# Seven-product pairs of a SwiGLU input stage: ScalarE's order (seed, SiLU, last difference), VectorE's first-pair order and two PSUM banks changed

## What is computed

```python
def swiglu(x, w_in, w_out):
    a, b = jnp.split(x @ w_in, 2, axis=-1)      # w_in: 1024 x 5632
    return (jax.nn.silu(a) * b) @ w_out
for i in range(2):
    h = h + 0.5 * swiglu(rmsnorm(h, g_ff1[i]), w_ff1_in[i], w_ff1_out[i])
    ...
    h = h + 0.5 * swiglu(rmsnorm(h, g_ff2[i]), w_ff2_in[i], w_ff2_out[i])
```

## Time and profile before

| | us |
|---|---|
| median of 3 runs | 2997.67 (2995.54 to 3002.64) |
| profiled execution, its own time | 2998.98 |
| its span | 2997.0 |
| TensorE busy / VectorE / ScalarE / GpSimd | 2900.9 / 2123.1 / 1396.3 / 455.9 |
| mean granted TensorE clock, share of full | 0.988 |

### The profile page before, as it was taken

One profiled execution on the slowest core, in us unless ns is written; L12 is line 12 of the kernel. 1 busy time (PEld: TensorE's weight loads), 2 busy tenths in 40 slices (PEclk: granted clock), 3 DMA queues, 4 the chain that ended last, 5 costly groups with the idle time before them and its releaser, 6 DMA issues. The chain is left out here.

```text
span 2997.0 us, 50791 instructions
## 1 busy us (share of the span) xinstructions
PE 2900.9 (97%) x18548; PEld 2500.2 (83%) x18548; DVE 2123.1 (71%) x3185; ACT 1396.3 (47%) x2309; POOL 455.9 (15%) x356
## 2 busy tenths in 40 slices
PE   7999999889999999999999999999999999999998
PEld 3888888777789988777799988799888777899886
DVE  5677776355689745887699845899547886899545
ACT  3645555454356522334466522566323335566422
POOL 0113112184600011000300012100110000200012
PEclk9999999999999999999999999999999999999998
DMA  6212022123223222322232323233222222323322
GB/s 258 62 44 63 24 55 59 36 81 117 99 88 112 97 98 81 98 92 77 98 107 98 115 88 112 71 112 99 100 89 92 92 78 87 110 98 112 104 95 74
DMA packets 97244, 275.10 MB, mean 92 GB/s; under 512 B 35712, under 2 KB 36864, under 8 KB 95760
## 3 DMA queue, kind: packets, MB, share of 16 engines
q1 hardware_dynamic: 94016, 267.89, 27.3%
q10 hardware_dynamic: 2768, 4.25, 0.5%
q0 software_dynamic: 320, 1.05, 0.1%
HBM read 267.88 MB, written 5.28 MB: 91 GB/s over the span
## 5 line engine op out<-in xcount | busy, mean ns | idle before, releaser
L142 DVE TENSOR_TENSOR weights_lo<-weights_raw,weights_hi 128x1024 fp32r<-128x1024 f32 (+2 forms) x258 | 397.6, 1541 | 326.2 <-ACT weights_hi L137 322.7
L137 ACT ACTIVATE weights_hi<-weights_raw 128x1024 fp32r<-128x1024 f32 (+2 forms) x250 | 285.3, 1141 | 431.8 <-PE bank L151 424.7
L149 PE MATMUL bank<-x_hi,weights_hi 128*128 128x512 f32 x832 | 336.9, 405 | 4.6 <-DVE x_lo L1943 2.7
L151 PE MATMUL bank<-x_hi,weights_lo 128*128 128x512 f32 x832 | 326.4, 392 | 0.0
L150 PE MATMUL bank<-x_lo,weights_hi 128*128 128x512 f32 x832 | 325.2, 391 | 0.0
L2053 PE MATMUL bank<-sum_hi,block_hi 128*128 128x256 f32 x960 | 271.2, 282 | 13.7 <-ACT bank L2194 9.6
L149 PE MATMUL bank<-hidden_hi,weights_hi 128*128 128x512 f32 x704 | 273.9, 389 | 0.0
L150 PE MATMUL bank<-hidden_lo,weights_hi 128*128 128x512 f32 x704 | 273.9, 389 | 0.0
L151 PE MATMUL bank<-hidden_hi,weights_lo 128*128 128x512 f32 x704 | 273.9, 389 | 0.0
L2054 PE MATMUL bank<-sum_lo,block_hi 128*128 128x256 f32 x960 | 270.8, 282 | 0.0
L2055 PE MATMUL bank<-sum_hi,block_lo 128*128 128x256 f32 x960 | 269.9, 281 | 0.0
(11 more groups left out here) (437 smaller groups left out, 7322.6 us busy)
## 6 DMA issues: line engine op xcount, KB each, us to landing
raw_pair<-w_ff1in SPq DMA_DIRECT2D x42, 1024.0 KB, 4.9
raw_pair<-w_ff2in SPq DMA_DIRECT2D x42, 1024.0 KB, 4.9
weights_raw<-w_mix SPq DMA_DIRECT2D x72, 512.0 KB, 3.5
weights_raw<-w_ff1out SPq DMA_DIRECT2D x32, 704.0 KB, 4.0
weights_raw<-w_ff2out SPq DMA_DIRECT2D x32, 704.0 KB, 4.1
weights_raw<-w_tail SPq DMA_DIRECT2D x42, 512.0 KB, 3.5
mod_weights<-w_mod SPq DMA_DIRECT2D x6, 2048.0 KB, 16.7
weights_raw<-w_dn SPq DMA_DIRECT2D x24, 512.0 KB, 3.7
```

The source lines that it names most:

```text
L137: nc.scalar.activation(K.wh[:, slot, 0:cols], K.raw[:, slot, 0:cols], ACT.Copy).then_inc(S.wh_ready, 1)
L142: nc.vector.tensor_tensor(K.wl[:, slot, 0:cols], K.raw[:, slot, 0:cols], K.wh[:, slot, 0:cols].bitcast(F32), ALU.subtract).then_inc(S.raw_ ...
L149: nc.tensor.matmul(out, K.wh[:, slot, a:b], xh, start=start, stop=False)
L151: return nc.tensor.matmul(out, K.wl[:, slot, a:b], xh, start=False, stop=stop)
```

## The change

ScalarE's order in each pair becomes seed, SiLU, `fourth_hi`. Pair 3 is taken out of the loop (`second=True`) with the order seed, (for q = 0 the second plain pair's SiLU, `plain_block_hi`, `hidden_hi`), `fourth_hi`, SiLU. The third and fourth plain slabs collect in banks 5 and 3 instead of 3 and 5. On VectorE `second` of pair 3 comes ahead of `first_lo`. For q = 0 both engines' first pairs get an order of their own: `rstd` right after the differences, the gates of the plain pairs later, the table load behind `plain_block_hi`. The table's SiLU writes a column of its own.

```diff
--- before.py
+++ after.py
@@ -319,6 +319,7 @@
     K.ident = put("identity", [128, 128])
     K.ones = put("ones", [128, 128])
     K.eps = put("eps", [128, 1])
+    K.unread = put("unread", [128, 1])
     K.banks = ctx.enter_context(nc.psum_tensor("bank", [128, 4096], F32))
     K.pb = [K.banks[:, 512 * i:512 * i + 512] for i in range(8)]
     return at
@@ -2038,14 +2039,14 @@
         if q > 0:
             pe_sum_squares(pe, q)
         project(1, 4, False)
-        project(2, 3, False)
+        project(2, 5, False)
         if q == 0:
             pe_sum_squares(pe, q)
             K.final_pe(pe)
 
         for bank in (1, 2):
             nc.tensor.matmul(pb[bank][:, :], K.identr[:, :], xgh[:, 0, :], start=True, stop=True)
-        project(3, 5, False)
+        project(3, 3, False)
 
         def product(out, hi, lo, x, start=False):
             for k in range(4):
@@ -2149,7 +2150,7 @@
             nc.scalar.activation(K.t1[:, :], K.t1[:, :], ACT.Silu).then_inc(S.silu_ready, 1)
 
         def silu_table():
-            nc.scalar.activation(K.s5[:, 0:1], K.eps[:, 0:1], ACT.Silu)
+            nc.scalar.activation(K.unread[:, 0:1], K.eps[:, 0:1], ACT.Silu)
 
         def hidden_hi(j):
             act.wait_ge(S.g_ready, FT * f + j + 1 + CREDIT)
@@ -2203,10 +2204,19 @@
             act.wait_ge(S.product_done, left("product_done") + 5 * number(j) + product)
             nc.scalar.activation(half_out(p, name), half_out(p, "a_right"), ACT.Copy).then_inc(S.seeded, 1)
 
-        def half_pair(j, p, end=False):
-            fourth_hi(j)
-            silu(j - 1)
-            seed_a(j, p)
+        def half_pair(j, p, end=False, second=False):
+            if second:
+                seed_a(j, p)
+                if q == 0:
+                    silu(1, True)
+                    plain_block_hi(j, p)
+                    hidden_hi(1)
+                fourth_hi(j)
+                silu(j - 1)
+            else:
+                seed_a(j, p)
+                silu(j - 1)
+                fourth_hi(j)
             keep_fifth(j)
             seed_b(j, p, "b_left", 3)
             hidden_hi(j - 1)
@@ -2224,6 +2234,20 @@
 
             first_hi(j, p, True)
             plain_block_hi(j, p)
+            if q == 0:
+                silu_table()
+                second_hi(j, True)
+                seed_a(j, p)
+                silu(0, True)
+                keep_fifth(j, True)
+                sum_hi(4)
+                seed_b(j, p, "b_left", 3)
+                fourth_hi(j)
+                seed_b(j, p, "b_right", 5)
+                first_hi(j + 1, 1 - p)
+                hidden_hi(0)
+                second_hi(j + 1)
+                return
             silu(0, True)
             second_hi(j, True)
             seed_a(j, p)
@@ -2249,9 +2273,12 @@
             act_std(act, q)
             K.final_act(act)
         sum_hi(3)
-        silu_table()
+        if q > 0:
+            silu_table()
         first_half_pair(PLAIN_PAIRS, 0)
-        with act.Fori(0, HALF_PAIRS // 2 - 1) as i:
+        half_pair(PLAIN_PAIRS + 1, 1, second=True)
+        half_pair(PLAIN_PAIRS + 2, 0)
+        with act.Fori(1, HALF_PAIRS // 2 - 1) as i:
             for p in (1, 0):
                 half_pair(2 * i + PLAIN_PAIRS + 2 - p, p)
         half_pair(FT - 1, 1, end=True)
@@ -2311,13 +2338,13 @@
         def scale_plain(j):
             dve.wait_ge(S.slab_done, s0 + 2 * j + 1 + CREDIT)
             dve.wait_ge(S.g_ready, FT * f + j + CREDIT)
-            nc.vector.tensor_tensor(K.t1[:, :], pb[3 * j][:, :], rstd[:, :], ALU.mult).then_inc(S.evac, 2)
+            nc.vector.tensor_tensor(K.t1[:, :], pb[5 * j][:, :], rstd[:, :], ALU.mult).then_inc(S.evac, 2)
 
         def gate_plain(j):
             dve.wait_ge(S.slab_done, s0 + 2 * j + 2 + CREDIT)
             dve.wait_ge(S.silu_ready, FT * f + j + 1 + CREDIT)
             dve.wait_ge(S.hid_ready, FT * f + j + CREDIT)
-            nc.vector.tensor_tensor(K.t2[:, :], pb[4 + j][:, :], K.t1[:, :], ALU.mult).then_inc(S.g_ready, 1)
+            nc.vector.tensor_tensor(K.t2[:, :], pb[4 - j][:, :], K.t1[:, :], ALU.mult).then_inc(S.g_ready, 1)
 
         def sum_b(j, p, end=False):
             dve.wait_ge(S.slab_done, s0 + 2 * j + (2 if end else 1) + CREDIT)
@@ -2398,13 +2425,34 @@
         def first_half_pair(j, p):
 
             differences(j, p)
+            if q == 0:
+                dve_rstd(dve, q, v0)
+                first_lo(j, p)
+                second(j, p)
+                fourth(j, p)
+                scale_plain(0)
+                second_lo(j)
+                plain_block_lo(j, p)
+                sum_lo(3)
+                sum_lo(4)
+                fourth_lo(j)
+                differences(j + 1, 1 - p)
+                gate_plain(0)
+                first_lo(j + 1, 1 - p)
+                second(j + 1, 1 - p)
+                scale_plain(1)
+                hidden_lo(0)
+                second_lo(j + 1)
+                gate_plain(1)
+                fourth(j + 1, 1 - p)
+                hidden_lo(1)
+                sum_b(j, p)
+                scale_a(j, p)
+                return
             second(j, p)
             fourth(j, p)
-            if q == 0:
-                first_lo(j, p)
             dve_rstd(dve, q, v0)
-            if q > 0:
-                first_lo(j, p)
+            first_lo(j, p)
             scale_plain(0)
             plain_block_lo(j, p)
             gate_plain(0)
@@ -2416,8 +2464,8 @@
             sum_lo(4)
             differences(j + 1, 1 - p)
             fourth_lo(j)
+            second(j + 1, 1 - p)
             first_lo(j + 1, 1 - p)
-            second(j + 1, 1 - p)
             fourth(j + 1, 1 - p)
             hidden_lo(1)
             second_lo(j + 1)
```

## The result

The changed kernel takes 3024.05 us (median; 3020.7 to 3025.27) against 2999.26 for the kernel before (four runs of it, among them the three of the table above), a ratio of 1.0081 with a 95% interval of 1.0064 to 1.0099. The forecast was 2985.0, range 2980.7 to 2991.5. The profiled execution's span is 3021.9 us, 24.9 more than before.

The account below looks back on a forecast made before the run. TensorE, busy 97% of 2997.0 us, bounds the kernel, so only its idle time and slow clock can be won. Gains 5.0 + 2.0 + 3.7 + 2.0 = 12.7 us give 2986.3, less 1.31 for the median 2985.0; range 2980.7 to 2991.5.

Parts of the forecast that it names:

- The waits: Second seven-product pairs and first stage: shorter TensorE waits, gaining 2.0 us in stages 2 and 4, 3.7 in 3, 5.0 in 1.
- PLAIN of pair 3 in stage 1: First stage: PLAIN starts at 844.45 after a new 3.2 us wait on `plain_block_lo`, 6.05 us earlier than before.
- The wait on `plain_block_lo`: Second pair of the three later stages: PLAIN, due at 1527.9, gets a new wait of 0.35 us.
- the 2.39: Second stage, pair 3: SECOND's 2.39 us wait for the seed, which stands behind SiLU, is gone with seed first.
- The slow clock: Half-clock stretch of 3.4 us costs 1.7: charged behind stage 1's new PLAIN wait, gone behind stage 3's second pair.
- The repeated pairs' waits: 72 loop pairs: no TensorE wait, nothing gained or lost; VectorE's idle 0.89 ahead of `second_lo` shrinks to 0.2.
- rival 4: Repeated pairs: gate behind SiLU behind seed, VectorE's cover too thin, 27.5 us lost less 12.7, 3012.5 us; chance 0.04.
- Rival 1: First stage: the new PLAIN wait brings no slow clock, gain 14.4, 2983.3 us; chance 0.18.
- rival 3: Three later stages: VectorE, not the seed, sets SECOND or PLAIN, waits of about 2 remain, gain 5.0, 2992.7 us; chance 0.08.
- rival 2: First stage gives all back through VectorE's single file and missed ScalarE handovers; gain 7.7, 2990.0 us; chance 0.12.
- The table load: First stage, ScalarE: load counted as 1.28 us without the skill's 1.38 drain, which would make the gain 4.7.

Follow-up runs that it names:

- run 2: Changed kernel with all its new order, its extra column moved to free bytes at the top of SBUF: 2988.39 us, ratio 0.9958 to the kernel before.
- run 4: Changed kernel with its extra column widened from 32 to 64 bytes: 2986.19 us, ratio 0.9957 to the kernel before.
- run 9: Changed kernel with its 32-byte column allocated ahead of the weights' buffers instead of behind them: 2982.03 us, ratio 0.9938 to the kernel before.
- run 10: As run 2, with the weights of all seven products at 64 modulo 128: 2963.53 us, ratio 0.9863 to the kernel before.
- run 11: As run 2, with the weights of all seven products at 0 modulo 128: 2990.91 us, ratio 0.9965 to the kernel before.
- run 1: Kernel before plus only an unused 32-byte column behind `eps`, shifting every buffer allocated after it: 3034.68 us against 2999.83, ratio 1.012.
- run 3: Kernel before plus an unused 64-byte column behind `eps`: 3001.73 us, ratio 1.0009.
- run 5: Kernel before with 32 bytes free ahead of `weights_raw`, moving the weights' buffers and everything behind them together: 2997.31 us, ratio 0.9994.
- run 6: Kernel before with only `x_hi` and `x_lo` at 32 modulo 64, all else moved by 0 or 64 bytes: 3020.93 us, ratio 1.007.
- run 7: Kernel before with `block_hi` and `block_lo` moved from 32 to 0 modulo 64 (64 modulo 128), order unchanged: 2981.34 us, ratio 0.9939.
- run 8: Kernel before with only the loop's new ScalarE order, also in pair 3, and the bank swap, memory unshifted: 2992.31 us, ratio 0.9975.

## Why the prediction was wrong, step by step

**The waits: right.** Run 2 shows them without the memory shift. In stages 2 and 4 the start of pair 4 lies 2.24 and 2.28 us earlier behind the stage's first product than before (20.42 for 22.66 and 22.70), 2.0 forecast; in stage 3 3.76 (20.43 for 24.19), 3.7 forecast; in stage 1 5.07 (25.30 for 30.37), 5.0 forecast. PLAIN of pair 3 in stage 1, the longest chain of the prediction, starts 18.00 behind the stage's first product; the prediction's own times give 844.45 - 826.4 = 18.05. Sum 13.3 in the trace, 12.6 in the ratio, 12.7 forecast. Stage 2's second pair in the changed kernel, ScalarE and VectorE, answers to the earlier trace rows:
```profile
1533.87 1.22 DVE L2398 TENSOR_TENSOR block_lo<-differences,block_hi 128x1024 fp32r<-128x1024 f32 x1
...
1534.54 0.58 ACT L2195 ACTIVATE bank<-bank 128x512 f32<-128x512 f32 x1 [1.01 <-PE bank L2056]
...
1536.21 1.22 DVE L2393 TENSOR_TENSOR plain_block_lo<-raw_pair,plain_block_hi 128x1024 fp32r<-128x1024 f32 x1
1536.33 0.63 ACT L2150 ACTIVATE t<-t 128x512 f32<-128x512 f32 x1 [0.67 <-DVE t L2357]
```
The seed no longer stands behind SiLU, and `second_lo` runs in time. The wait on `plain_block_lo`, 0.35 forecast, stands in run 2's timeline as 0.15. The timeline counts idle time from the modelled end of the last matmul, 0.16 after the next one would normally have started, so PLAIN is 0.31 late. The same 0.16 is missing in the 2.39, which delayed SECOND by 2.55; that is why 2.24 was gained where I had summed 2.0.

**The slow clock: right in place, too dear in price, and in stage 3 partly luck.** In stage 1 the wait of 2.92 is followed by one stretch at half clock, as charged; the one behind stage 3's second pair is gone. From the changed kernel's timeline, and its granted clock behind the wait (columns as in the earlier trace rows):
```profile
848.53 0.38 PE L2054 MATMUL bank<-x_hi,plain_block_hi 128*128 128x256 f32 x1 [2.92 <-DVE plain_block_lo L2393]
```
```profile
849.40:852.80 3.40, 3.40 (x18) 3.40 (x18) 3.37 (x7) 1.41 (x2) 0.00 (x0) 0.51 0.91 296
```
That charge was sound: a wait of 2.9 us there comes with one slow stretch in all six traces with the new order of stage 1 (the change, runs 2, 4, 9, 10, 11). Its price was not. I took half of 3.4 us, but by the earlier trace rows the stretch holds 18 or 19 matmuls where 29 fit, so about 10 are lost, 1.2 us; by pair times it costs 1.53 (24.19 - 22.66 before, stage 3 against stage 2). In stage 3 the 0.2 charged too much and the 0.24 of the waits that I had missed cancel, which is why 3.7 met 3.76. And that stage 3 had a slow stretch at all was the draw of one execution: in the six traces that keep the old order (before, runs 1, 3, 5, 6, 7) 10 of the 18 waits on the seed in stages 2 to 4 come with one, from none in run 7 to all three in runs 5 and 6. The 13.3 is a difference from that same trace, so its closeness to 12.7 says less than it seems; the 12.6 from the run times, 9.3 to 16.2, is the independent figure.

**The repeated pairs' waits: right.** Run 2 and the change have no TensorE wait in the loop. VectorE's idle time ahead of `second_lo` fell from 0.89 to 0.18, where 0.2 was forecast, and the gate waits for SiLU instead; another pair of the changed kernel:
```profile
1602.13 1.23 DVE L2398 TENSOR_TENSOR block_lo<-differences,block_hi 128x1024 fp32r<-128x1024 f32 x1 [0.18 <-ACT block_hi L2185]
...
1606.38 0.69 DVE L2362 TENSOR_TENSOR t<-t,t 128x512 f32<-128x512 f32 x1 [0.69 <-ACT t L2150]
```
So rival 4, the only one on the slower side, named the wrong mechanism, though the sign was its own. Rival 1 (no slow clock) and rival 3 (the swap not working) did not happen either; rival 2's chain stayed in time.

**The table load: right by the row.** In the changed kernel too the load (827.88, 1.28 us) is followed at once by the next ACTIVATE:
```profile
827.88 1.28 ACT L2153 ACT_TABLE_LOAD   x1
829.17 0.20 ACT L2153 ACTIVATE unread<-eps 128x1 f32<-128x1 f32 x1
```
The Trainium skill (ScalarE: Activation LUTs, section What ACT_TABLE_LOAD costs) counts 1.38 us of drain on top of the load for every switch to another set. This trace does not agree: 0.01 us lies between the load's end and the next start.

**What failed** is the step that isn't there. Every line of order was priced, the line that allocates was not: I took a column that is never read for free, and said of the loop that no instruction's kind changes, which is true. The sum then has terms for the second pairs and the first stage only, as if the 0.118 us a matmul, and every matmul outside the four stages, would stay as they were. The first became 0.1194 (10.03 / 84), and 226.7 ns became 233.3 in code the diff doesn't touch. Price of the missing term: +35 us by run 1. With it the sum would have been 12.7 gained and 35 lost, 3020; measured 3024. No row shown ahead of the prediction gives this price; only a run that moves the buffers does.

## What to carry to other kernels
A new buffer in the middle of a hand-made memory map is an edit to every buffer behind it: put it at the end or in a gap, or pad so that the distance modulo 64 between weights and moving operands stays (modulo 128, where the 1% between 226.7 and 229 ns counts). When a change alters no work but a trace shows TensorE busy longer at full clock, compare start-to-start spacing in a stage the diff doesn't touch, before looking for waits. And try a few placements of the weights on an already tuned kernel: here one of them (block weights at 64 modulo 128, run 7) gave 18 us without touching any order, more than the reordering. At 256 columns the addresses alone did not tell the outcome, so measure it, and more than once.

## What the runs showed that was not expected
- The float32r matmul's spacing depends on where weights and moving operand start: 226.7, 229 or 233.3 ns at 512 columns for distances 0, 64 and 32 modulo 128; independent of what VectorE, ScalarE, GpSimd and the DMA engines do.
- At 256 columns there are several levels between 113 and 121 ns, the lowest only at distance 64, and one program with fixed addresses can run its stages at different ones (run 10: pairs of 9.52 and of 9.89 us, and runs spread over 18 us, where the others spread over 4 to 13; run 9: the plain products at 117.9 in stage 1 and 113.8 in the others). What chooses the level stays open; it was not tried with weights and moving operand in isolation.
- The same wait of 2.4 us comes with a slow stretch in one execution and not in the next (10 of 18), which cost 1.5 us where it was measured; the waits of 0.6 in run 8 came with none (0 of 4).
